# Prompt attention moved by half a sequence in the decode of a recurrent and attention decoder step, with 34 identity products among TensorE's last waits

## The reference

```python
def fox_attention(q, k, v, f_q, f_k, q_pos, k_pos):      # per block of queries
    s = einsum('bqhd,bkhd->bhqk', q_i, k) * scale
    s = s + f_i[..., None] - f_key                       # forget gates
    s = where(k_pos <= pos_i, s, -inf)
    p = softmax(s, axis=-1)
    return einsum('bhqk,bkhd->bqhd', p, v)
h = h + (fox_attention(...) @ fox_w_o)                    # "fo", then the last SwiGLU
```

## Time and profile before

| | us |
|---|---|
| median of 3 runs (lowest, highest) | 1598.87 (1596.99, 1603.84) |
| the profiled execution | 1605.04 |
| its span, first to last instruction | 1603.0 |
| TensorE busy in the span | 1537.2 |
| VectorE, ScalarE, GpSimd busy | 966.1, 664.2, 123.9 |
| mean granted TensorE clock, of full speed | 0.972 |
| decode, from the last product of `q` to the last 128 columns of `fo` | 1133 to 1330 |

### The profile page before, as it was taken

The page is one execution under the profiler, slowest core; times in us unless marked ns, Lnnn a source line. Parts: engine busy times, 40 slices in busy tenths (PEclk is TensorE's granted clock), DMA queues, the critical chain, the costliest instruction groups (busy, mean ns, idle before and its releaser), DMA issues.

```text
span 1603.0 us, 34107 instructions
## 1 busy us (share of the span) xinstructions
PE 1537.2 (96%) x14044; PEld 1431.4 (89%) x14044; DVE 966.1 (60%) x1395; ACT 664.2 (41%) x1029; POOL 123.9 (8%) x182
## 2 busy tenths in 40 slices
PE   8999999998999999999999999999887889999998
PEld 8999997997888899999999999999643449999998
DVE  6655437686896575554467655445766665655532
ACT  5434325554656544433343443333333333533321
POOL 0000000002322100000002440000011110000000
PEclk9999999999999999999999999999889898999999
DMA  8665682430100566656765544447599983444442
GB/s 270 226 232 191 220 241 73 147 106 15 30 17 18 163 224 227 217 192 229 237 198 186 164 144 150 145 145 279 205 351 345 336 331 125 150 140 156 150 146 79
DMA packets 241003, 288.52 MB, mean 180 GB/s; under 512 B 18898, under 2 KB 221922, under 8 KB 240754
## 3 DMA queue, kind: packets, MB, share of 16 engines
q1 hardware_dynamic: 237234, 281.20, 52.3%
q0 software_dynamic: 3648, 5.57, 1.3%
HBM read 280.39 MB, written 39.90 MB: 200 GB/s over the span
## 4 chain that ended last, share of the span: by engine, by line
PE 84%; DVE 7%; DMA 4%; ACT 2%; issue 1%; SPq 1%; POOL 0%; DVEq 0%; ACTq 0%
PE ps L739 23%; PE ps L740 23%; PE ps L741 23%; PE ps L1040 4%; DMA arena<-in_cache_v 3%; PE ps L1035 3%; PE ps L1487 1%; PE ps L793 1%; DVE ring L2719 1%; DVE ring_r L2118 1%; DMA ring<-in_fox_w_o 1%; DVE arena L2271 1%; PE ps L1066 1%; PE ps L1175 1%; PE ps L1191 1%
## 5 line engine op out<-in xcount | busy, mean ns | idle before, releaser
L739 PE MATMUL ps<-arena_r,ring_r 128*128 128x320 f32 (+1 forms) x2016 | 627.9, 311 | 1.9 <-DVE xn_r L2118 1.9
L741 PE MATMUL ps<-arena_r,ring_r 128*128 128x320 f32 (+1 forms) x2016 | 625.3, 310 | 0.0
L2118 DVE TENSOR_TENSOR ring_r<-ring,ring_r 128x2048 fp32r<-128x2048 f32 (+2 forms) x131 | 291.4, 2226 | 249.6 <-ACT ring_r L1610 144.8
L739 PEld LDWEIGHTS ps<-arena_r,ring_r 128*128 128x128 f32 x2016 | 382.0, 189 | 6.1 <-issue 3.2
L741 PEld LDWEIGHTS ps<-arena_r,ring_r 128*128 128x128 f32 x2016 | 382.0, 189 | 0.0
L740 PE MATMUL ps<-arena_r,ring_r 128*128 128x320 f32 x1136 | 351.7, 310 | 0.0
L740 PE MATMUL ps<-xn_r,ring_r 128*128 128x320 f32 (+2 forms) x880 | 273.7, 311 | 0.0
L740 PEld LDWEIGHTS ps<-arena_r,ring_r 128*128 128x128 f32 x1136 | 213.8, 188 | 0.2
L2118 DVE TENSOR_TENSOR arena_r<-arena,arena_r (+3 forms) x155 | 141.9, 926 | 109.9 <-ACT arena_r L1610 48.9
L739 PE MATMUL ps<-arena_r 128*128 128x320 f32 x592 | 183.2, 309 | 0.0
L741 PE MATMUL ps<-arena_r 128*128 128x320 f32 x592 | 182.9, 309 | 0.0
(11 more groups left out here) (377 smaller groups left out, 1841.2 us busy)
## 6 DMA issues: line engine op xcount, KB each, us to landing
ring<-in_ffn_w_in SPq DMA_DIRECT2D x66, 1024.0 KB, 5.1
k_grouped<-in_cache_k SPq DMA_DIRECT2D x64, 512.0 KB, 5.4
arena<-in_cache_v SPq DMA_DIRECT2D x64, 512.0 KB, 7.9
ring<-in_ffn_w_out SPq DMA_DIRECT2D x24, 1024.0 KB, 5.1
ring<-k_grouped SPq DMA_DIRECT2D x44, 512.0 KB, 6.6
arena<-in_ffn_w_in SPq DMA_DIRECT2D x21, 1024.0 KB, 5.1
ring<-in_rw_w_rkv SPq DMA_DIRECT2D x11, 1024.0 KB, 5.1
arena<-k_grouped SPq DMA_DIRECT2D x20, 512.0 KB, 8.1
```

The costliest lines, as they stand in the source:

```text
L739: pe.matmul(out, part(s, 1)[:, k, cs], x_hi, start=first_, stop=False)
L741: return pe.matmul(out, part(s, 0)[:, k, cs], x_hi, start=False, stop=last)
L2118: return TT(out, x, high.bitcast(F32), ALU.subtract)
```

## The change

Prompt head work is placed elsewhere in each iteration, and everything else in the iteration is written around it.

- TensorE: `fox_turn`, `fox_values` of heads 2b-2 and 2b-1 are now in iteration b instead of b-1, ahead of `page_outputs(b-1, 0)`; `fox_scores(2b)` comes behind four of these pages, `fox_scores(2b+1)` behind all of them, just ahead of `unit_scores(b, 3)`. `turn_output` writes to `P_TURNED[0]` instead of a bank of the scores. In the last part 34 products of the identity with itself (`keep_warm`) into an unused bank: 6 behind each of the two last `fox_turn`, 2 ahead of each of the nine `page_outputs`, 4 behind them.
- VectorE: pages 0 and 1 of sequence b+1 are turned behind `scaled_output(b-1)` and ahead of `fox_scored(2b+1)`, `half_max(b)` and `less_max(b)`; pages 2 and 3 stay behind `less_max(b)`. The masks of the new tokens are made among the query scalings, before the loop.
- ScalarE, GpSimd: `fox_exp`, `fox_columns`, `fox_out`, `probabilities` and `out_low` follow in the new order. In the last iteration `fox_exp(15)` and `fox_sums(15)` come behind `output_columns(6)` and `less_max(7)`.
- The queue of SyncE is unchanged.

```diff
@@ TensorE
             unit_scores(0, 0)
-            head_groups("k_own", kT)
+            unit_scores(0, 1)
             pe.wait_ge(S("q_rn"), 2)
             query_rep("q_rep", P, 2, rs[:, TS:TS + P])
-            unit_scores(0, 1)
             unit_scores(0, 2)
+            head_groups("k_own", kT)
             fox_scores(0)
+            unit_scores(0, 3)
+            own_scores(0)
             fox_scores(1)
-            for b in range(BS):
-                last = b == BS - 1
-                if b:
-                    fox_scores(2 * b)
-                    unit_scores(b, 0)
-                    turn_probabilities(b - 1)
-                    unit_scores(b, 1)
-                    fox_scores(2 * b + 1)
-                    for j in range(4):
-                        page_outputs(b - 1, j)
-                    unit_scores(b, 2)
-                    for j in range(4, PAGES + 1):
-                        page_outputs(b - 1, j)
-                if not last:
-                    fox_turn(2 * b)
+            for b in range(1, BS):
+                unit_scores(b, 0)
+                fox_turn(2 * b - 2)
+                unit_scores(b, 1)
+                turn_probabilities(b - 1)
+                fox_turn(2 * b - 1)
+                fox_values(b - 1)
+                for j in range(4):
+                    page_outputs(b - 1, j)
+                fox_scores(2 * b)
+                unit_scores(b, 2)
+                for j in range(4, PAGES + 1):
+                    page_outputs(b - 1, j)
+                fox_scores(2 * b + 1)
                 unit_scores(b, 3)
                 own_scores(b)
-                if not last:
-                    fox_turn(2 * b + 1)
-                    fox_values(b)
-                if b:
-                    turn_output(b - 1)
+                turn_output(b - 1)
+            def keep_warm(n):
+                for _ in range(n):
+                    pe.matmul(ps[:, SCORES[0][1], 0:P], ident, ident, start=True, stop=True)
             b = BS - 1
             fox_turn(2 * b)
+            keep_warm(6)
             fox_turn(2 * b + 1)
+            keep_warm(6)
             turn_probabilities(b)
             fox_values(b)
             for j in range(PAGES + 1):
+                keep_warm(2)
                 page_outputs(b, j)
+            keep_warm(4)
@@ VectorE
+            for b in range(1, BS):
                 last = b == BS - 1
...
+                turn_page(b, 2)
+                turn_page(b, 3)
+                fox_sums(2 * b - 1)
+                turn_page(b, 4)
+                turn_page(b, 5)
+                probability_sums(b - 1)
+                turn_page(b, 6)
+                turn_page(b, 7)
+                fox_scored(2 * b)
+                scaled_output(b - 1)
                 if not last:
                     turn_page(b + 1, 0)
                     turn_page(b + 1, 1)
+                fox_scored(2 * b + 1)
+                fox_sums(2 * b)
+                half_max(b)
+                less_max(b)
+            fox_sums(2 * BS - 1)
```

More of the change, by code:

```diff
@@ L149, in plan_tiles @@
     add("q_own", 1, "a")
+    add("q_rep", DT // 2)
     add("k_own", 1, "a")
-    add("q_rep", DT // 2)
     add("fo", DT)
@@ L1383, in turn_probabilities @@
                     if b:
-                        pe.wait_ge(S("pT_ready"), 3 * b - 2 + half)
+                        pe.wait_ge(*((S("pT_ready"), 3 * b - 1) if half else (S("o_out"), 2 * b)))
                     for m in range(4):
@@ L1435, in fox_scores @@
                     pe.wait_ge(S("nF_ready"), 1)
-                    dve_done(first["q_rep"])
+                    dve_done(first["q_rep"] + 1)
                 pr = halves_of[e]
@@ L1475, in unit_scores @@
                         pe.wait_ge(S("p_row"), (b - 2) * 3 + u // 2 + 1)
-                        pe.wait_ge(*((S("pT_ready"), 3 * (b - 1)) if u else (S("o_out"), 2 * (b - 1))))
+                        if u:
+                            pe.wait_ge(S("pT_ready"), 3 * (b - 1))
                 pe.wait_ge(S("page_turned"), b * PAGES + 2 * u + 2)
@@ L1497, in own_scores @@
                     pe.wait_ge(S("pT_ready"), 3 * b - 1)
-                else:
-                    dve_done(first["q_rep"] + 3)
                 for e in range(2):
@@ L2036, in output_columns @@
                     act.activation(oT[pr, :, b * QS + TP:(b + 1) * QS + TP].rearrange("p (g c) q -> p g c q", g=4),
-                                   ps[pr, SCORES[b % 2][0], 0:P].rearrange(
+                                   ps[pr, P_TURNED[0], 0:P].rearrange(
                                        "p (c e g q) -> p e g c q", c=2, e=2, g=4)[:, e_], ACT.Copy
@@ L2056, in _ @@
             own_columns("q_own", q_f)
+            past_forget(0, 1)
             own_columns("k_own", kT)
-            for b in range(BS):
+            past_forget(1, 0)
+            fox_exp(0)
+            for b in range(1, BS):
                 last = b == BS - 1
[L2060 to L2064, removed]
+                fox_exp(2 * b - 1)
+                fox_columns(2 * b - 2)
+                page_exp(b - 1, 0)
+                page_exp(b - 1, 1)
+                own_exp(b - 1)
                 past_forget(b, 1)
-                fox_exp(2 * b)
-                fox_exp(2 * b + 1)
+                probability_copy(b - 1)
+                fox_columns(2 * b - 1)
+                fox_out(b - 1)
                 if not last:
                     past_forget(b + 1, 0)
-                    fox_columns(2 * b)
-                    fox_columns(2 * b + 1)
-                    fox_out(b)
                 else:
                     hi(first_slab["fo"])
-                if b:
-                    output_columns(b - 1)
+                fox_exp(2 * b)
+                output_columns(b - 1)
+            fox_exp(2 * BS - 1)
             b = BS - 1
@@ L2757, in _ @@
             query_reciprocal("q_norm_s", 0, TS)
+            dve.memset(mask_new.rearrange("p b k -> p (b k)"), NEG).then_inc(S("mask_step"), 1)
             sample_scaled()
+            dve.wait_ge(S("mask_step"), 1)
+            for b in range(BS):
+                ins = CP(mask_new[:, b, b * QS:(b + 1) * QS], K("new"))
+            ins.then_inc(S("mask_step"), 1)
             filled(first["q_own"])
@@ L2763, in _ @@
             query_reciprocal("q_norm", TS, P)
+            dve.wait_ge(S("mask_step"), 2)
+            link(TT(mask_new, mask_new, F_row.unsqueeze(1).to_broadcast([P, BS, TS]), ALU.subtract))
             def fox_scored(hd):
@@ L2811, in scaled_output @@
                 dve.tensor_reduce(o_sum, o_own.rearrange("p g d -> p d g"), AX.X, ALU.add).then_inc(S("o_sum"), 1)
[L2813 to L2820, removed]
-                last = b == BS - 1
[L2822 to L2846, removed]
-                    new_masks()
-                less_max(b)
+            for j in range(4, PAGES):
+                turn_page(0, j)
+            prompt_scaled(0)
+            prompt_scaled(1)
+            turn_page(1, 0)
+            turn_page(1, 1)
+            fox_scored(0)
+            prompt_scaled(2)
+            prompt_scaled(3)
+            fox_scored(1)
+            half_max(0)
+            less_max(0)
+            fox_sums(0)
+            for b in range(1, BS):
+                last = b == BS - 1
+                turn_page(b, 2)
[8 more added lines that the diff above has]
+                scaled_output(b - 1)
                 if not last:
@@ L2981, in _ @@
             pool.wait_ge(act_freed, freed["a"][first["q_own"] + 1])
-            for b in range(BS):
+            queries(1)
+            probabilities(0)
+            for b in range(1, BS):
+                probabilities(2 * b - 1)
                 if b + 1 < BS:
                     queries(b + 1)
+                out_low(b - 1)
                 probabilities(2 * b)
-                probabilities(2 * b + 1)
-                if b + 1 < BS:
-                    out_low(b)
+            probabilities(2 * BS - 1)
             pool.wait_ge(S("shift_stored"), 32)
```

3 lines of the change are left out of this document (1 added, 2 removed).

## The result

The changed kernel takes 1602.87 us in the median of 12 runs (1600.36 to 1606.36); the kernel before, run beside it, 1597.35 us (12 runs, 1593.91 to 1604.52). The ratio is 1.0033, 95% interval 1.0017 to 1.0048: 5.3 us slower, or 5.5 by the medians. A second set of runs of the same two kernels gave 1.0039 (1.0024 to 1.0054); one of its ten runs of the changed kernel took 2635 us at a mean clock of 0.707 and is left out of every comparison. The forecast was 1597.5, hence no change. The time lies in its range and within 0.5% of before, but on the slower side, and beyond what the measurement leaves open.

What follows compares the result with a forecast made beforehand. Loop held by a ring of TensorE, VectorE and ScalarE, hardly shorter than the loads' ring. Terms -3 - 2.6 + 10.5 - 6.3 = -1.4 us, put on the median: 1597.5; 8-in-10 range from 1586 to 1608, half of each end's rival left out.

Steps and rivals of the forecast that it cites:

- What bounds it: Whole kernel: the change acts only on the decode, some 200 of 1603 us, and the dense last stage's start.
- the loop: Decode iterations: a turn takes 22.9 us instead of 23.8, five turns gain 2.6 us; 12.1 at full clock.
- Start: Decode start, with masks moved into waits: outputs of sequence 0 end 0 to 4 us earlier, taken as 3.
- Tail: From sequence 5's outputs to `fo`'s last 128 columns: they start 10.5 us later, about 5 from identity products.
- Clock at `fo`: Last 128 columns of `fo`: TensorE's clock stays full after a shorter gap, -6.3 us; if not, 0.
- The median: Whole kernel: runs' median is 6.2 us below the profiled execution, and the forecast difference is applied to it.
- Rival 2: Last outputs: identity products run at half clock, +8.9 us, 1608; chance 0.18 together with worse tail sums.
- Rival 4: Tail: identity products fail, gap and clock as before, +4.9 us, 1603.8; counted inside the forecast's 0.55.
- Rival 3: Loop: transfers become the bound, turn 22.6 to 23.7 us, at worst +1.1, 1600; inside the forecast's 0.55.
- the skill's rule: Loop transfers: memory side binds at about 358 GB/s, turn not under 23.4 us, no loop gain, about 1600.

Runs made afterwards that it cites:

- e2: Changed kernel without its 34 identity products; ratio to the kernel before 1.0032.
- e3: Changed kernel with only the twelve identity products behind the two last `fox_turn`, the other 22 removed; ratio to the kernel before 1.0001.
- e8: Changed kernel with the edits of e5 and e7 together; ratio to the kernel before 0.9894, median 1583.43 us.
- e6: Changed kernel, products kept, with VectorE's split of slab 0 moved behind `probability_sums(7)`; ratio to the kernel before 1.0009.
- e7: Changed kernel, products kept, with TensorE's scores of pages 2 and 3 moved behind `turn_probabilities`; ratio to the kernel before 0.9966.
- e5: Changed kernel without its 34 products, with three tail moves: VectorE's slab 0 split later, two reorderings on ScalarE; ratio to before 0.9956, median 1590.84 us.
- changed again: Changed kernel, no edit, run and profiled a second time; ratio to the kernel before 1.0039.
- e11: Changed kernel without its 34 products, with four in the gap ahead of the last 128 columns of `fo`; ratio to before 0.9983.
- before again: Kernel before, no edit, run again for its second profile; ratio to the kernel before 1.0013.
- e4: Kernel before with the same 34 identity products in the same places of its tail; ratio to the kernel before 1.0019.
- e9: e8 plus four identity products in the gap ahead of the last 128 columns of `fo`; ratio to before 0.9889, median 1580.27 us.
- e12: Kernel before with seven identity products in the gap ahead of the last 128 columns of `fo`; ratio to before 0.9958.

## Why the prediction was wrong, point by point

- **What bounds it, and the loop: right.** "I take 22.9 us" for a turn: 22.6. The clock fell at the end of the stretch that I named, the waits for value pages went, and TensorE waits for page turns and the copy ahead of `fox_values`. The gain was 4.2 us against the first profile and 2.0 against the second, where 2.6 was forecast.
- **Start: right in kind.** 37.8 us to the outputs of sequence 0 against 41.2 to 42.3: 3.4 to 4.5, forecast 3.
- **Tail: the step that failed.** "**10.5 later** than before" became 14.9 against the first profile and 15.6 against the second. Two terms were mis-sized. "An identity product is ... 0.22 us" holds in a row of six (1.34 us for x12 above), but not in pairs between outputs on other buffers: 0.32 each, and a page's outputs 0.57 instead of 0.46; outputs with their products took 11.8 us instead of 8.1 + 0.9. "GpSimd (... an estimate of 1.1 to 1.2 for all of it)" took 3.0, because VectorE's split now runs beside it; I had not asked who works beside it. 2.8 and 1.9 make 4.7, and the miss is 4.4 us against the first profile and 5.1 against the second.
- **Clock at `fo`: the number right, the reason not.** It is right for the first profile to a tenth (272.8 to 266.5, -6.3), with some luck: its two parts were 4.9 and 1.4 instead of 5.1 and 1.2. Against the second profile it is 4.8. But I took it that the clock stays because the gap gets shorter than 1.92 us. Without the products it fell behind gaps of 0.89 (e2, e3) and 0.80 us (e8); the shorter gap alone does not keep it.
- **The median: wrong.** "I put the difference on the median." Against the second profile of before, whose time (1596.30) is near the median, the stretches give 0.1 - 3.4 - 2.0 + 15.6 - 4.8 = +5.5, and +5.3 was measured. Against the means of the profiles that have before's code in a stretch they give -4.1 - 3.6 + 15.3 - 5.5 = +2.1. So some 3 us are not settled. Of the 100 runs of before 21 took under 1595 us, with a mean clock of 0.9783, and 26 over 1600 us, with 0.9735, so more or less half clock is a part of its spread. None of the 21 was profiled; whether they lack the fall at `fo`, or their turns, which wait for transfers, are shorter, no run here shows.
- **Rival 2 (identity products at half clock)** did not occur: 1.00 from 1311 on. Its sign, slower, came true by other terms, not by its own. Rival 4, that the products don't keep the clock, was true in one of five executions with all 34 (e6).
- **Rival 3 and the skill's rule.** The loop of e7 moves 400 GB/s over 110 us, so the memory side's 358 GB/s that the Trainium skill, "DMA: Bandwidth & Descriptors", section on where 436 GB/s comes from, lets bind does not hold for this one core; the measurement decides.

So the new loop and start were worth 5 to 9 us, and the tail cost 15. Of that, 6.6 were the products (e2) and 1.8 the collision of GpSimd and VectorE (e6). Another 2.2 are what is left of e5's 4.0, which I put down to the order of ScalarE's last steps; no run moves these alone. Some 5 remain, and I put them down to the last sequence's scores and probabilities, which stand behind the outputs of the one before it. That is argued and not shown: no run moves them back, and 2.9 of the 5 went when the loop's move of the scores was added (e8, 39.3 against 42.2).

## What to carry to other kernels

Put filling work into the gap itself, not in front of it, and count its cost in the place where it stands: four products in the gap gave what 34 elsewhere gave, for nothing. When a loop is reordered, walk its last turn on its own, with every engine's queue and what runs beside what. And take at least two profiles of the kernel before: where the single one lies above its median, the excess may be in the very terms that the change gains on.

## What the runs showed of the hardware that was not expected

- GpSimd's multiplication of 128x128 took 0.40 us alone and 2.37 us beside a VectorE subtraction of 128x2048 with two inputs on chip: it was held for nearly all of that instruction's 2.27 us. It took 2.37 us in all six profiles in which the two run side by side (changed, changed again, e2, e3, e7, e11), and 0.40 in the other eight. VectorE's own time did not grow (2.27 against 2.29).
- TensorE's clock fell some 1.6 to 2.5 us after a pause of only 0.80 to 1.5 us, into a stretch that was busy without a gap, and stayed at 0.50 for 10.2 us in each of five profiles (before again, e2, e3, e6, e8). In the first profile of before it fell at the end of a pause of 1.92 us and stayed for 13.7. It is not decided by the instructions alone: with the same 34 products and the same gap of 0.89 us it stayed in four kernels' profiles (changed, changed again, e4, e7) and fell in one (e6). With the gap closed or filled it stayed in four of four (e5, e9, e11, and e12, where 0.35 us of it was left).
- A pair of 128x128 products between the outputs of two pages took 0.64 us, six in a row 1.34 us, both at a granted clock of 1.00.
